# A hybrid decoder layer on one core: the value product of the attention turned around and rounded, and split weights kept in memory for later strips

## What is computed

```python
h = rms_norm(x, norm_pre_mix); proj = h @ w_in               # 2048 tokens, width 1024
q, k, v, qi, ki, wi, hq, hf, hi, hg = split_columns(proj)    # rope on q, k, qi, ki
# group A: 8 query heads x 64, 2 shared key/value heads
iscore = einsum('btsh,bth->bts', relu(qi . ki), wi)          # 8 indexer heads, causal
idx = top_k(iscore, 256)
s = where(valid, (q . k[idx]) * 64 ** -0.5, -inf); p = softmax(s); o = p @ v[idx]
# group B: gated linear recurrence (HGRN2), chunkwise
mix = concat(att_out, hg_out) @ w_out
x = x + rms_norm(mix, norm_post_mix); h2 = rms_norm(x, norm_pre_ffn)
ff = (silu(h2 @ w_gate) * (h2 @ w_up)) @ w_down              # width 2816
x = x + rms_norm(ff, norm_post_ffn)
```

## Time and profile before

| | |
|---|---|
| median of 3 runs | 3363.66 us (3360.87 to 3364.05) |
| the profiled execution | 3365.06 us, its span 3363.2 us, mean granted clock 0.985 |
| TensorE (PE) | busy 3208.6 us, 95% |
| VectorE (DVE) | busy 2267.8 us, 67% |
| ScalarE (ACT) | busy 1500.0 us, 45% |
| GpSimd (POOL) | busy 239.5 us, 7% |
| DMA | 345.66 MB, mean 103 GB/s |

### The profile page before, as it was taken

How to read it: one execution, slowest core, us unless ns; L and a number is a source line. 1 busy time by engine, 2 the same in 40 slices (tenths; PEclk the granted TensorE clock), 3 DMA queues, 4 the chain that set the end, 5 groups by cost and what they waited for, 6 DMA issues and landing times.

```text
span 3363.2 us, 46512 instructions
## 1 busy us (share of the span) xinstructions
PE 3208.6 (95%) x18048; PEld 2833.5 (84%) x18048; DVE 2267.8 (67%) x3817; ACT 1500.0 (45%) x2477; POOL 239.5 (7%) x400
## 2 busy tenths in 40 slices
PE   8999999999899899999989999998999999989998
PEld 8999999998777788888778888887888888868886
DVE  4467777788566766676787777777876775464444
ACT  3455445455456544344554444445454444333222
POOL 0000000000111110010100001011100000010000
PEclk9999999999899999999989999999999999999999
DMA  5543343344323222222522112134211212252233
GB/s 183 169 130 125 132 150 113 126 132 131 107 86 111 97 84 84 73 72 72 187 78 75 65 63 84 63 111 148 69 63 60 66 56 68 101 178 97 88 107 107
DMA packets 147500, 345.66 MB, mean 103 GB/s; under 512 B 15056, under 2 KB 35920, under 8 KB 145232
## 3 DMA queue, kind: packets, MB, share of 16 engines
q1 hardware_dynamic: 144976, 338.49, 30.3%
q10 hardware_dynamic: 2304, 4.20, 0.3%
HBM read 283.31 MB, written 59.31 MB: 102 GB/s over the span
## 4 chain that ended last, share of the span: by engine, by line
PE 63%; DVE 6%; ACT 2%; issue 2%; DMA 1%; DVEq 0%; SPq 0%; POOL 0%; ACTq 0%; POOLq 0%
PE PJ_d L2070 9%; PE PJ_d L2072 9%; PE PJ_d L2071 9%; PE SC L2026 6%; PE PJ_d L2095 6%; PE PJ_d L2097 6%; PE PJ_d L2096 6%; PE SA L1985 3%; PE SA L2012 3%; PE SA L1986 3%; PE SA L1981 1%; DVE wd_lo L1826 1%; DVE score L1717 1%; DVE prob L1811 1%; DVE h_lo L1831 1%
## 5 line engine op out<-in xcount | busy, mean ns | idle before, releaser
L2070 PE MATMUL PJ_d<-h_hi,wd_hi 128*128 128x512 f32 (+1 forms) x1472 | 576.9, 392 | 14.8 <-DVE h_lo L1831 9.9
L2072 PE MATMUL PJ_d<-h_hi,wd_lo 128*128 128x512 f32 (+1 forms) x1472 | 564.5, 384 | 0.0
L2071 PE MATMUL PJ_d<-h_lo,wd_hi 128*128 128x512 f32 (+1 forms) x1472 | 563.8, 383 | 0.0
L1580 ACT ACTIVATE wd_hi<-wd_raw 128x512 fp32r<-128x512 f32 x568 | 344.7, 627 | 225.1 <-DMA wd_raw<-in_w_gu 128.7
L733 PE MATMUL PJ<-w_hi,h_hi 128*128 128x338 f32 (+1 forms) x1280 | 415.9, 325 | 2.7 <-DVE w_lo L550 2.7
L1826 DVE TENSOR_TENSOR wd_lo<-wd_raw,wd_hi 128x512 fp32r<-128x512 f32 x568 | 380.3, 689 | 44.3 <-ACT wd_hi L1580 41.1
L734 PE MATMUL PJ<-w_lo,h_hi 128*128 128x338 f32 (+1 forms) x1280 | 408.6, 319 | 0.0
L735 PE MATMUL PJ<-w_hi,h_lo 128*128 128x338 f32 (+1 forms) x1280 | 408.4, 319 | 0.0
L1575 ACT ACTIVATE pT<-SA 128x512 f32<-128x512 f32 (+3 forms) x320 | 156.5, 531 | 508.6 <-PE SA L2012 508.4
L1811 DVE CUSTOM_DVE_ANT_0 prob<-SA,bias 128x1024 f32<-128x1024 f32 (+7 forms) x192 | 170.1, 911 | 300.5 <-PE SA L1986 296.8
L2070 PEld LDWEIGHTS PJ_d<-h_hi,wd_hi 128*128 128x128 f32 x1472 | 280.8, 191 | 65.7 <-DVE wd_lo L1826 6.1
(11 more groups left out here) (207 smaller groups left out, 5725.2 us busy)
## 6 DMA issues: line engine op xcount, KB each, us to landing
wd_raw<-in_w_gu SPq DMA_DIRECT2D x352, 256.0 KB, 2.9
wd_raw<-in_w_down SPq DMA_DIRECT2D x176, 256.0 KB, 2.6
w_raw<-in_w_in SPq DMA_DIRECT2D x40, 684.0 KB, 4.5
w_raw<-in_w_in SPq DMA_DIRECT2D x40, 676.0 KB, 4.5
row_h<-proj_d SPq DMA_DIRECT2D x16, 1024.0 KB, 7.2
proj_d<-stage SPq DMA_DIRECT2D x40, 342.0 KB, 4.6
proj_d<-stage SPq DMA_DIRECT2D x40, 338.0 KB, 5.1
x_d<-acc SPq DMA_DIRECT2D x24, 512.0 KB, 2.9
```

The source lines that it names most:

```text
L1580: s_.activation(w_hi[:, u % RING, :], w_raw[:, u % RING, :], ACT.Copy).then_inc(w_hi_ready, 1)
L2070: t.matmul(to[:, tok], w_hi[:, r, w], h_hi[:, c, tok], start=(c == 0 and part != 1), stop=False)
L2071: t.matmul(to[:, tok], w_hi[:, r, w], h_lo[:, c, tok], start=False, stop=False)
L2072: last = t.matmul(to[:, tok], w_lo[:, r, w], h_hi[:, c, tok], start=False, stop=(c == KD - 1 and part != 0))
```

## The change

1. **The value product.** V becomes the weights: a tile of 128 keys x 128 holds the high and the low part of one value head's 64 columns. The turned probabilities are split too (ACT writes the high part, DVE the low one, a new instruction in `turned_probs_low`) and move as 256 columns, high and low. One rounded matmul per 128 keys and head gives a 128 x 256 result with all four partial products, in which the output stands turned. ACT copies the half from the low probabilities to `oT`, DVE adds the other half (`add_output`), and TensorE turns it back and adds the rows of high and low V in one plain fp32 product against a folded identity (`turn_output`, one head behind). Two heads at a time are divided and stored (`attention_pair`, `store`).
2. **V in memory.** POOL splits the values of a block, SP stores them to `v_d`, and for each block and value head SP loads what the product needs, in chunks of 4 key blocks, into one set of four tiles (`load_values`), which from block 4 on serves both value heads one after the other.
3. **Split weights in memory.** Strip 0 stores each of its 140 split units, high and low side by side, to `split_d` (512 KB each); strips 1, 2 and 3 load them from there, and neither ACT nor DVE splits them again.
4. **Queries.** Two heads are turned in one transpose of 128 columns. ACT and DVE split even and odd heads apart. Rows come in two loads (`load_rest`, `load_q`) into one buffer, and POOL rotates them in two parts.
5. Small tiles (`wis`, `nmx`, `den`, `ss`, `rstd` and others) stand now at the end of the old `xt` buffer; the order listing names them `xt`.

```diff
+SPLIT_KEPT = (1, 2, 3)
...
+        if unit[0] != "part" and unit[1] == 0:
+            kept_at[same] = len(kept_at)
+            home[unit] = u
+            users[u % RING] += 1
+            stored_no[u] = users[u % RING]
+        if unit[0] == "part" or unit[1] not in SPLIT_KEPT:
+            split_no[u] = len(split_no)
...
+                if u - RING in stored_no:
+                    sp.wait_ge(split_stored[u % RING], 16 * stored_no[u - RING])
+                if u not in split_no:
+                    first = keeper(u)
+                    sp.wait_ge(split_stored[first % RING], 16 * stored_no[first])
+                    at = kept_at[(kind,) + units[u][2:]]
+                    sp.dma_start(w_two[:, u % RING].bitcast(F32), split_d[at]).then_inc(w_in[u % RING], 16)
+                    return
...
+            def store_split(u):
+                sp.wait_ge(w_lo_ready, split_no[u] + 1)
+                at = kept_at[(units[u][0],) + units[u][2:]]
+                sp.dma_start(split_d[at], w_two[:, u % RING].bitcast(F32)).then_inc(split_stored[u % RING], 16)
...
+            def load_values(b, g):
+                sp.wait_ge(v_stored, 16 * (b + 1))
...
+                for c in range(NCH(b)):
+                    if v_before[b, g, c]:
+                        sp.wait_ge(pv_done, v_before[b, g, c])
...
+                    sp.dma_start(v_tiles[n][:, k:k + last - 4 * c, :].bitcast(F32), v_d[g, :, 4 * c:last, :]).then_inc(v_loaded[b, g, c][0], 16)
...
-                    s_.activation(pT[:, m % 2, 0:w], pair(("pT", b, h, p))[:, 512 * (c % 2):512 * (c % 2) + w], ACT.Copy)\
-                      .then_inc(pt_ready, 1)
+                    of = pair(("pT", b, h, p))[:, 512 * (c % 2):512 * (c % 2) + w]
+                    s_.activation(pT[:, m % 2, 0:w // P, 0, :], heads(of, w // P), ACT.Copy).then_inc(pt_ready, 1)
+
+            def copy_low_output(b, h):
...
+                s_.activation(oT[:], SC[:, P:2 * P], ACT.Copy).then_inc(ot_half, 1)
...
+            def turned_probs_low(b, h, p):
...
+                    dve.wait_ge(pt_ready, m + 1)
...
+                    v.tensor_tensor(to[:, :, 1, :], heads(of, w // P), to[:, :, 0, :].bitcast(F32), ALU.subtract).then_inc(pt_low, 1)
+
+            def add_output(b, h):
+
+                dve.wait_ge(ot_half, HEADS * b + h + 1)
+                v.tensor_tensor(oT[:], SC[:, 0:P], oT[:], ALU.add).then_inc(ot_ready, 1)
...
                     fill(("A", b, h))
+                    for j in pairs_turned(b, h):
+                        attention_pair(b, j)
+                    turned_probs_low(b, h, 0)
...
                     for k in search(b, h, "A"):
                         topk_part(b + 1, k)
                     fill(("B", b, h))
+                    if pairs_of(b) == 2:
+                        turned_probs_low(b, h, 1)
...
-                    pe.wait_ge(pt_ready, m + 1)
+                    pe.wait_ge(pt_low, m + 1)
...
-                        last = t.matmul(SC[:, h * HD:(h + 1) * HD], pT[:, m % 2, (kb % 4) * P:(kb % 4 + 1) * P],
-                                        V[:, kb, g * HD:(g + 1) * HD], start=(kb == 0), stop=(kb == b))
+                        last = t.matmul(SC[:, 0:2 * P], values_of(b, g, kb),
+                                        pT[:, m % 2, kb % 4].rearrange("p n t -> p (n t)"), start=(kb == 0), stop=(kb == b))
...
+            def turn_output(b, h):
...
+                t.matmul(SC[:, 2 * P + n % 2 * HD:2 * P + (n % 2 + 1) * HD], oT[:], folded, start=True, stop=True)\
+                 .then_inc(ot_turned, 1)
```

More of the change, by code:

```diff
@@ L953, in mixer_phase, with keeper @@
                 unit_last[unit_no[u]] = n
+    kept_at, home, split_no, stored_no, users = {}, {}, {}, {}, [0] * RING
+    for u, unit in enumerate(units):
+        same = (unit[0],) + unit[2:]
+        if unit[0] != "part" and unit[1] == 0:
[5 more added lines that the diff above has]
+            split_no[u] = len(split_no)
+    def keeper(u):
+        return home[(units[u][0], 0) + units[u][2:]]
     loads_after, split_step = {}, dict(enumerate((0, 0, 1, 1, 3, 4, 5, 6)))
@@ L1177, in pair, with rows_of, of_parity @@
             return SA[:, use[key] % 2, :]
+        def rows_of(key):
+            return HD if key[0] == "keys" else P
+        def of_parity(ap, odd):
+            return ap.rearrange("p (j two) t -> p j two t", two=2)[:, :, odd, :]
+        highs_upto = []
+        for key in hi_order:
+            highs_upto.append((highs_upto[-1] if highs_upto else 0) + (1 if key[0] == "keys" else 2))
         pair_read = []
@@ L1699, in low @@
                 else:
[L1700 removed]
+                    to = qT if what == "q" else qiT
                     if what == "q" and b >= 1:
@@ L1704, in low @@
                         dve.wait_ge(doubled["qi"], b - 2)
-                    v.scalar_tensor_tensor(to[:, 1], heads(pair(key)[0:HD], 8), -SM_SCALE if what == "q" else 1.0,
-                                           to[:, 0].bitcast(F32), ALU.mult, ALU.subtract).then_inc(sa_free_dve, 1)
+                    for odd in range(2):
+                        at = slice(odd * HD, (odd + 1) * HD)
+                        last = v.scalar_tensor_tensor(of_parity(to[0:HD, 1], odd), heads(pair(key)[at, 0:4 * P], 4),
+                                                      -SM_SCALE if what == "q" else 1.0,
+                                                      of_parity(to[at, 0], odd).bitcast(F32), ALU.mult, ALU.subtract)
+                    last.then_inc(sa_free_dve, 1)
             def accumulate(b, c, h):
@@ L1975, in open_split @@
                 if b >= 1:
-                    pe.wait_ge(rows_ready, b)
+                    pe.wait_ge(q_ready if what == "q" else rest_ready, b)
                 first = ((K0, K0 + HD, KI0) if what == "keys" else
-                         [(Q0 if what == "q" else QI0) + h * HD for h in range(HEADS)])
+                         [(Q0 if what == "q" else QI0) + j * P for j in range(HEADS // 2)])
                 take(key)
                 for h, c0 in enumerate(first):
-                    last = t.transpose(pair(key)[0:HD, h * P:(h + 1) * P], row[:, b % 2, c0:c0 + HD], ident[:])
+                    last = t.transpose(pair(key)[0:rows_of(key), h * P:(h + 1) * P], row_of(b)[:, c0:c0 + rows_of(key)],
+                                       ident[:])
                 last.then_inc(sa_full, 1)
@@ L2135, in _ @@
                         turn_probs(b, h, p)
+                        if p == 0 and h >= 1:
+                            turn_output(b, h - 1)
                         fill(("BC"[p], b, h))
                         values(b, h, p)
-            for n in range(*TAIL):
+            item(TAIL[0])
+            turn_output(NB - 1, HEADS - 1)
+            for n in range(TAIL[0] + 1, TAIL[1]):
                 item(n)
```

326 lines of the change are left out of this document (239 added, 87 removed).

## The result

| | before | after |
|---|---|---|
| median | 3363.43 us (4 runs) | 3468.37 us (4 runs, 3466.25 to 3472.64) |
| span of the profiled execution | 3363.2 us | 3464.5 us |
| TensorE busy, idle | 3208.6, 154.6 us | 3178.5, 286.0 us |
| DVE, ACT, POOL busy | 2267.8, 1500.0, 239.5 us | 2228.4, 1312.8, 263.2 us |
| mean granted clock | 0.985 | 0.967 |

The change makes the kernel slower: ratio 1.0315, 95% interval 1.0302 to 1.0328. The forecast was 3283.

A forecast was written before the change was run, and what follows sets the result against it. The prediction took TensorE to bound the kernel. Its terms, -91 + 20 - 22 + 12 = -81 from the profiled 3365.1, gave 3284 us, stated as 3283 against the median, with a range of 3243 to 3335.

The forecast's parts named there:

- TensorE's own sum: TensorE's pace: value product -104, turning back +28, queries -12, fewer switches between plain and rounded matmuls -3; in all -91 us.
- turning back: TensorE's 128 plain fp32 products, two instructions each at 0.108: +28 us; they wait for DVE's addition, but one head behind.
- The queries' -12: On TensorE, 240 query transposes become 120 at 0.097 us each: -12 us.
- The new wait: TensorE's value product waits for DVE's low part in 192 calls; 0.8 us fits into 1.46 free: +12, bounds 0 to 132.
- Strip 0's load: Up to 1641 all splits stay and DVE's load rises to some 79%: +20 us, bounds 0 and 148.
- The relief: Without weight splits on DVE and ACT after strip 0, TensorE's holes at strip meetings shrink: -22 us.
- Rival 5: The relief is larger: some 80 us of TensorE's holes after 1200 halve, giving 3243 us; chance 0.11.
- Memory and SP: Doubled weight loads, strip 0's stores and SP's in-order waits cost zero, up to some 10 us in the range.
- Rivals 3 and 4: Doubled weights arrive late, 3367 us, chance 0.01; value product's weights don't load beside the matmul before, 3490 us, chance 0.01.
- Rival 1: DVE becomes the bound, the value product's new wait sitting behind DVE's search: slower, 3421 us; chance 0.04.

The follow-up runs named there:

- e11: e1 plus queries turned in pairs, nothing of the new value product, against the kernel before: 3361.75 us, ratio 0.9998.
- e3: The changed kernel with low parts of the turned probabilities left zero, never computed; TensorE waits for ACT's high parts: 3396.81 us, ratio 1.0097.
- e4: The changed kernel without turning back: ACT's copy, DVE's addition, TensorE's product and their waits gone, DVE divides a constant: 3395.48 us, ratio 1.0093.
- e9: e5 with DVE work of the same shapes as low parts and additions put back, from constants, nobody waiting for it: 3321.88 us, ratio 0.9876.
- e5: The changed kernel with the edits of e3 and e4 together, neither low parts computed nor outputs turned back: 3295.90 us, ratio 0.9791.
- e1: The kernel before with only the kept split weights added (strip 0 stores, strips 1 to 3 load): 3361.92 us, ratio 0.9994.
- e2: The changed kernel without kept weights, every strip splitting anew, plus one more wait on POOL: 3489.48 us, ratio 1.0372.
- e12: The changed kernel in full; ACT copies both output halves, TensorE adds them while turning back; from block 8 second low part precedes search parts: 3446.33 us, ratio 1.0248.

## Why the prediction was wrong

- **TensorE's own sum, -91.** Right: the pace sum fell by 106. The 256 columns go at 0.12 as forecast. One term in it is off, turning back: 0.14 us for two instructions, 18 us for all, not 28. The queries' -12 is real on TensorE, but e11 shows none of it at the end.
- **The new wait, +12.** This step failed. I wrote that the 0.8 us of the low part fit into the 1.46 free in the earlier trace rows, with "a halving is 2.35 us" as the longest thing ahead. That is a middle part of the search. Its last part stands in slot A of head 7, and the trace of before had it at 2415.86 with two rounds of MAX8 and MATCH_REPLACE8. I priced the wait from one quiet head, as a small one for each of 192 calls. The trace shows 26 waits, 56 us in sum and up to 7.6 long; blocks 8 and 12, where strips meet, have 37 of the 56, and head 7 has 28. With their wake, and with the load that the low parts are for DVE, they are worth 72 us (e3).
- **Turning back, "one head behind" and no wait.** The second failure. I costed that wait at nothing because of the distance of a head. In blocks 0 to 3 the order does not have this distance: the output is turned back at the top of the next head, right behind its own product where slot B is empty, and TensorE waits 25 us there. And head 7's output has no next head in any block: it follows in the first indexer product of the next block, and DVE's addition stands behind the end of the search and the dense work, 17 us in all. It is worth 73 us less some 18 of pace (e4). The division, which the value product waits for since it shares a bank, was costed as DVE time alone; TensorE waits 20 us for it.
- **Strip 0's load, +20.** Nearer right as a load: all of DVE's new work costs 26 us where nobody waits, 11 of it by the start of block 8 (1670 in e9, 1659 in e5). What the load adds while the two chains wait behind it no run shows by itself.
- **The relief, -22.** The mechanism is wrong. On the kernel before e1 measures nothing, inside some 5 us. I also read the earlier trace rows wrongly: its 16 waits are 8 stops, each counted for the matmul and for its weight load. TensorE itself was idle 11.5 us in them, 4 of these before 1641. Most of the rest went in e1, and the wait for `acc` grew by 7. In the changed kernel the relief is worth 21 us (e2), near my 22, but by luck: it mostly shortens the waits for low parts, which I had not priced. Rival 5 goes with it.
- **Memory and SP, zero.** Right on the whole: e1 carries the stores and doubled loads at no cost, and in the changed kernel TensorE is busy for all of the 300 us from 3100. The late load of block 6 is an exception on the new chain. Rivals 3 and 4 fall too.
- **The clock.** Not costed at all. It fell from 0.985 to 0.967, and the longer steps at the low level make 37 us more.
- **Rival 1** named the right mechanism for blocks 8 to 15, the wait behind DVE's search, and came to 3421 with a chance of 0.04; it has nothing of the waits for the addition and the division. I held against it that DVE at 82% leaves no hole between 2400 and 2500. That row says how full DVE is, not how long it keeps one instruction waiting; in the kernel before the same 82% hid a queue of some 12 us (from 2415.86 on), for which TensorE had no need to wait.

What stays open: whether a full-precision order exists that beats the kernel before. e12 is the best found. Cutting the search's last part into pieces between heads was not tried.

## What to carry to other kernels

When an edit moves a short step of an in-order engine onto the bound engine's path, price it by the longest uninterrupted work that can stand ahead of it in any iteration, the last and the first included, not by a quiet iteration or by that engine's busy share. And read the distance that you count on ("one head behind") in the order of every kind of iteration: here the short blocks did not have it. Work put on the engine without a waiter cost 26 us here for 206 us of it; with TensorE and DVE waiting in the chains the same work cost 172, 18 of it TensorE's own new product. Relief of an engine that the bound engine seldom waits for was worth nothing here until it did wait.

## What was not expected of the hardware

- With new weights for each instruction, the pace of a rounded product is nearly flat from 256 down to 128 columns, 0.120 and 0.112 us by the medians of the steps, and a plain pass of 64 columns has 0.112 too, while 512 take 0.23. In this range it pays little to cut columns; fewer instructions pay.
- DVE never lets the low part past the search: with its input there at 2535.73 it starts at 2544.52. The Trainium skill (TensorE: Matmul & The Clock Gate, Architectural detail) says that ACT and DVE are strictly first in, first out; the trace agrees.
- Reading a number from a tile to branch on it costs DVE 0.87 us of idle time here (2537.25 to 2538.12), and 0.85 to 0.92 in the ten blocks where the profile names this wait:

```profile
2538.12 0.15 DVE L1983 TENSOR_SCALAR left<-left 128x1 f32<-128x1 f32 x1 [0.87 <-DVE left_int L1979]
```
